# Eighteen unread matmuls between two groups of transposes, at three passages of a decoder kernel

## What is computed

```python
for layer in range(DEPTH):
    h = rms_norm(x, norm_mix[layer])
    proj = h @ w_in[layer]
    ...
    x = x + mix @ w_out[layer]
    h = rms_norm(x, norm_ffn[layer])
    if layer % 2 == 0:
        x = x + swiglu(h, ffn_w1[li], ffn_w3[li], ffn_w2[li])
    else:
        x = x + moe_swiglu(h, router[li], moe_w1[li], moe_w3[li], moe_w2[li])
```

## Time and profile before

| | us |
|---|---|
| median of 3 runs | 2078.56 |
| lowest, highest | 2078.51, 2080.9 |
| the profiled execution, its time | 2078.5 |
| the profiled execution, its span | 2076.7 |
| TensorE matmuls busy | 2023.9 (97%) |
| VectorE busy | 1583.8 (76%) |
| ScalarE busy | 1252.3 (60%) |

### The profile page before, as it was taken

The page is one execution under the profiler, slowest core; times in us unless marked ns, Lnnn a source line. Parts: engine busy times, 40 slices in busy tenths (PEclk is TensorE's granted clock), DMA queues, the critical chain, the costliest instruction groups (busy, mean ns, idle before and its releaser), DMA issues.

```text
span 2076.7 us, 28711 instructions
## 1 busy us (share of the span) xinstructions
PE 2023.9 (97%) x10743; PEld 1727.8 (83%) x10743; DVE 1583.8 (76%) x1219; ACT 1252.3 (60%) x1068; POOL 13.9 (1%) x21
## 2 busy tenths in 40 slices
PE   9999999999999999999979999999999999999997
PEld 8887888789998987888768888888888888888885
DVE  5778865755445778855767898888989888898986
ACT  5655455443345655454446777777777777777774
POOL 0000000000000000000000000000000000000000
PEclk9999999999999999999989999999999999999998
DMA  8523455255554523455238999999999999999994
GB/s 276 162 82 102 143 181 183 82 182 184 182 183 158 168 80 109 145 177 177 93 141 317 380 354 382 367 361 377 359 379 355 381 367 360 376 359 377 358 373 182
DMA packets 240494, 516.60 MB, mean 249 GB/s; under 512 B 11520, under 2 KB 34296, under 8 KB 240414
## 3 DMA queue, kind: packets, MB, share of 16 engines
q1 hardware_dynamic: 238018, 507.39, 69.1%
q0 software_dynamic: 2144, 7.88, 1.0%
q10 hardware_dynamic: 252, 0.22, 0.0%
HBM read 513.34 MB, written 2.12 MB: 248 GB/s over the span
## 4 chain that ended last, share of the span: by engine, by line
PE 91%; DVE 4%; ACT 2%; issue 2%; DVEq 0%; ACTq 0%
PE PS L481 27%; PE PS L483 26%; PE PS L482 26%; PE PS L565 7%; PE PS L1054 1%; ACT hi L1165 1%; PE PS L1031 1%; DVE lo L1652 1%; PE PS L806 1%; PE PS L720 0%; PE PS L1001 0%; PE PS L837 0%; DVE t_n L1675 0%; PE PS L1019 0%; DVE b_gc L1982 0%
## 5 line engine op out<-in xcount | busy, mean ns | idle before, releaser
L1652 DVE TENSOR_TENSOR lo<-raw,hi 128x2048 fp32r<-128x2048 f32 x481 | 1095.8, 2290 | 299.7 <-ACT hi L1165 297.5
L1165 ACT ACTIVATE hi<-raw 128x2048 fp32r<-128x2048 f32 x481 | 919.6, 1915 | 320.0 <-PE PS L483 313.8
L481 PE MATMUL PS<-hi,e_hi 128*128 128x512 f32 x896 | 356.2, 398 | 1.4 <-DVE e_lo L1675 1.4
L483 PE MATMUL PS<-hi,e_lo 128*128 128x512 f32 x896 | 350.4, 391 | 0.0
L482 PE MATMUL PS<-lo,e_hi 128*128 128x512 f32 x896 | 350.0, 391 | 0.0
L481 PE MATMUL PS<-hi,actT_hi 128*128 128x512 f32 x640 | 253.8, 397 | 3.7 <-DVE lo L1652 3.1
L483 PE MATMUL PS<-hi,actT_lo 128*128 128x512 f32 x640 | 249.7, 390 | 0.0
L482 PE MATMUL PS<-lo,actT_hi 128*128 128x512 f32 x640 | 249.2, 389 | 0.0
L481 PE MATMUL PS<-hi,fT_hi 128*128 128x512 f32 x536 | 208.8, 390 | 1.8 <-DVE fT_lo L1675 1.8
L483 PE MATMUL PS<-hi,fT_lo 128*128 128x512 f32 x536 | 208.7, 389 | 0.0
L482 PE MATMUL PS<-lo,fT_hi 128*128 128x512 f32 x536 | 208.7, 389 | 0.0
(11 more groups left out here) (324 smaller groups left out, 2147.1 us busy)
## 6 DMA issues: line engine op xcount, KB each, us to landing
raw<-in_moe_w SPq DMA_DIRECT2D x336, 1024.0 KB, 5.5
raw<-in_w_in SPq DMA_DIRECT2D x92, 1024.0 KB, 5.1
raw<-in_ffn_w SPq DMA_DIRECT2D x33, 1024.0 KB, 5.3
raw<-in_w_br SPq DMA_DIRECT2D x12, 1024.0 KB, 5.0
raw<-in_w_out SPq DMA_DIRECT2D x8, 1024.0 KB, 5.0
hankel<-hankel_dram POOLq DMA_DIRECT2D x1, 1536.0 KB, 12.8
x<-in_x SPq DMA_DIRECT2D x2, 512.0 KB, 5.1
f_gain<-in_norm_ffn POOLq DMA_DIRECT2D x2, 512.0 KB, 3.7
```

The source lines that it names most:

```text
L481: pe.matmul(out, a_hi, b_hi, start=first, stop=False, skip_group_check=True)
L483: return pe.matmul(out, a_lo, b_hi, start=False, stop=last, skip_group_check=True)
L1165: act.activation(hi[prog.u % SPLIT][:, :], raw[slot][:, :], COPY).then_inc(hi_made.sem, 1)
L1652: dve.tensor_tensor(lo[prog.u % RAW][:, :], raw[prog.u % RAW][:, :], hi[s][:, :].bitcast(F32), ALU.subtract).then_inc(lo_made.sem, 1)
```

## The change

`turn_input` calls a new helper between the first tile's eight transposes and the wait for the second tile's norm, in all calls but the first (`mixer(0)`). The helper issues eighteen matmuls. Their stationary operand is the first 128 columns of `ab_hi` (the high part of three small weight matrices, 192 columns, made near the start of the kernel), their moving operand all 192 columns. Each starts and ends its own sum, in bank 7 where `b` = 0 (place B) and in bank 1 where `b` = 4 (places A and C). They wait for nothing of their own, they signal nothing, and no instruction reads what they write.

```diff
@@ -501,6 +501,8 @@
             pe.wait_ge(norm_made.sem, norm_made.at(L, 3 * phase))
             for k in range(KT):
                 turn(0, k)
+            if L or phase:
+                spare(7 if b == 0 else 1, 18)
             for half in range(2):
                 pe.wait_ge(norm_made.sem, norm_made.at(L, 3 * phase + 1 + half))
                 for j in range(2 * half, 2 * half + 2):
@@ -554,6 +556,12 @@
+        def spare(b, count):
+
+            w = ab_hi[:, :, :, :].rearrange("p a k n -> p (a k n)")
+            for _ in range(count):
+                pe.matmul(PS[:, b, 0:3 * KT * 8], w[:, 0:P], w, start=True, stop=True)
```

## The result

The changed kernel takes 2088.38 us (median of 5 runs, 2087.1 to 2094.24) where the kernel before takes 2078.51 us (5 runs, 2077.45 to 2080.9): a ratio of 1.0051, with a 95% interval of 1.0037 to 1.0064. That is slower by more than the 0.2% that a measurement of this kernel can tell, and above the range that was given.

The account below looks back on a forecast made before the run. The prediction took the kernel as bound by TensorE, its matmuls busy for 97% of 2076.7 us. Terms -1.94 (A), +2.8 (B) and 0.0 (C) gave +0.9 on 2078.5, so 2079.4 us, range 2077.6 to 2083.0.

Parts of the forecast that it names:

- B: Layer 1, first norm: added matmuls delay the second tile's transposes and the first product; +2.8 us, bounds +1.2 to +5.7.
- A: Layer 0, second norm: added matmuls fill TensorE's idle time, the clock level stays up, products run faster; -1.94 us.
- C: Layer 1, second norm, before the router: narrow product done 1.2 us sooner, nobody gains; 0.0 us, 0.8 either way.
- The sum over the three places: Whole kernel: -1.94 + 2.8 + 0.0 = +0.9 us on 2078.5, so 2079.4 us, chance 0.47.
- The price of one matmul: Each added matmul at all three places: 0.119 us at the upper clock level, 0.213 us at the lower.
- the dear bound: Each added matmul priced per column: 0.160 us upper level, 0.320 us lower; as a rival 2080.3 us, chance 0.12.
- the estimate by the formula of the Trainium skill: Each added matmul: 160 ns cold, 82.5 ns warm; about 0.6 us off B's cost, not used in the sum.
- the level falls at A all the same: Rival at A: the clock level drops despite the added matmuls, A gives only 0.10 us; 2081.2 us, chance 0.22.
- the level does not rise: Rival at B: lower clock under the added matmuls; 2082.3 us with A kept (0.08), 2084.1 with A lost (0.05).
- The fast rival: From C on: level stays up to the gather, gather and 12 products save 5.8 us; 2073.6 us, chance 0.03.
- The forecast is wrong if...: Three signs: level at A falls before 449, is still low at B's first product, or is full at the gather.

Follow-up runs that it names:

- e6: The kernel before with 27 tiny matmuls (54 instructions) ahead of the expert loop; 2082.26 us, 73 pieces of code fetched.
- e8: The kernel before with 110 tiny matmuls (220 instructions) ahead of the expert loop; no total time given, steps with a loop return 127.44 and 127.60 us against 121.08.
- e14: The kernel before with 123 tiny matmuls (246 instructions) ahead of the expert loop; no total time given, no loss at the loop returns.
- e2: The change plus 74 tiny matmuls ahead of the expert loop, 256 added instructions in all; 2081.53 us, ratio 1.0003 to the kernel before.
- e4: The change without the matmuls at B, plus 92 tiny ones ahead of the expert loop, 256 added instructions; 2077.74 us, ratio 0.9996 to the kernel before.
- e10: The kernel before with 124 tiny matmuls (248 instructions) ahead of the expert loop; no total time given, 56 pieces fetched, no loss at the loop returns.
- e1: The kernel before with 54 tiny matmuls (108 instructions, as many as the change adds) ahead of the expert loop; 2089.09 us, ratio 1.0048.
- e3: The kernel before with 54 tiny matmuls behind the expert loop, ahead of the last scatter; 2078.77 us, ratio 0.9994.
- e5: The kernel before with 10 tiny matmuls (20 instructions) ahead of the expert loop; no total time given, placement found good.
- e7: The kernel before with 90 tiny matmuls (180 instructions) ahead of the expert loop; no total time given, nine pieces fetched per later pass.
- e9: The kernel before with 14 tiny matmuls (28 instructions) ahead of the expert loop; no total time given, first loop return costs, second does not.
- e13: The kernel before with 11 tiny matmuls (22 instructions) ahead of the expert loop; no total time given, placement found good.
- e15: The kernel before with only the change's eighteen at B, plus 110 tiny matmuls, 256 added instructions; 2081.48 us, ratio 1.0008.
- e11: The change without B, eight more matmuls behind A's second tile, both router waits filled, 256 added instructions; 2077.65 us, ratio 0.9991 to the kernel before.
- e12: Like e11, with 22 matmuls at B ahead of the first tile's wait and the gap behind the gather filled; 2076.57 us, ratio 0.9988 to the kernel before.

## Why the prediction was wrong

**The sum over the three places.** It said +0.9 us; the stages give -0.36 + 2.76 + 0.21 = +2.6 us. That alone would have been 2081, inside the range.

*The price of one matmul* was right: 0.119 us (2.24 us for 18, of which the last takes about 0.2), and the dear bound is out. So is the estimate by the formula of the Trainium skill ("TensorE: Matmul & The Clock Gate", section "Wait — 56ns, not 53.3ns?"), 82.5 ns.

*A* was forecast at -1.94 with the level kept, and the rival "the level falls at A all the same" at -0.10. The change's profile has the rival, softened: the level fell, at 449.2, later and for half as long, and the stage is 0.36 us shorter. Even that is not the eighteen's doing for certain: e6, e8 and e14, whose first column is like the change's and which have nothing added at A, are shorter by 0.3 to 0.4. Both cases exist for the same code, as e2 and e4 show with -1.83 and -1.86. Where nothing is added at A, the stage goes with the first column of the table: -0.3 to -0.4 us where that is -0.9 to -0.6 (e6, e8, e14), 0 where it is 0 (before, e10), -1.2 to -1.4 where it is +3.3 to +3.6 (e1, e3, e5), and +0.3 to +0.5 where it is +3.7 to +3.9 (e7, e9, e13, e15). So what the level costs at A goes with what happened 420 us earlier; that one causes the other was not tried. The step that failed at A was to take one execution's loss of 1.84 us as what stands to be gained each time.

*B* was right in mechanism: the eighteen stand in front of the second tile's transposes and push the first product back, forecast 2.9 us, measured 2.9. The size, +2.8 forecast, is +2.76 in the change, +2.77 in e15, and +4.0 in e2, where the lower level lasted longer (its eighteen took 4.13 us). That it fits so well is partly luck, for what the stage does without them is not fixed either: -0.15 us in e1 and e3, +0.2 in e6, e8 and e14, +1.7 in e7, e9 and e13. Set against kernels with a like start, the eighteen cost 2.5 us in the change and 1.1 in e15. The rival "the level does not rise" didn't occur in the change. In e2 it half did: all eighteen ran at the lower level, and it was up again only by the first product.

*C* was right: 0.0 at VectorE's read, gather and twelve products at the lower level as before. The fast rival (level kept up to the gather) failed, and e11 and e12 show that even the waits as filled there do not bring it.

**The failed step is one that was never written.** The sum ended with "-1.94 + 2.8 + 0.0", which says that nothing changes anywhere else. The eighteen were costed as time on TensorE and never as code. Three calls are 108 instructions ahead of a loop that is 1763 long and whose code just stayed in place, and the returns of the loop, +6.77 us, are more than twice the whole rest. No rival, bound or row covered it, and the statement "The forecast is wrong if..." looked at three places only: none of its three signs came true (the level at A fell at 449.2, just behind the 449 that it names), and the forecast was wrong all the same. The rows for it were there: the page before counted 55 pieces of code, and the table of queues for the loop had none of them. A loop whose fetches stop after the first pass stays in place, and a kernel with such a loop has something to lose.

The Trainium skill, "Runtime: NRT & Kernel Launch", section "Instruction fetch mechanics", says that TensorE's instruction memory is a FIFO of 128 KiB, refilled in blocks of 256 instructions. It also says that a taken branch whose target lies outside a window of two pages waits until the target is fetched. The traces agree with the blocks (1.20 MB in 73 pieces) and with a wait at a branch (6.28 us at the first return, of which 3.2 reach the matmuls). They disagree with the window: before, a loop of 6.89 blocks was repeated with no fetch at all. My estimate from the page's 128 KiB: that is eight blocks, and if one of them is being filled, a loop of up to seven would stay. That would be 30 placements, near the 33 to 63 that the scan shows, and e13 and e14 say that it is not the whole rule.

That the change's loss in the loop is the placement of the code is shown: e1 has the loss without the matmuls, e2 has the matmuls without the loss, e3 has the code behind and no loss. Why one return costs 1.8 us and another 5 to 6.5 the traces show for the most part. The 5.0 us at the change's first return are the stop of 3.2 us plus the lower level behind it (some 8 products at 0.2 us), while behind the second, shorter stop of 1.6 us its level stays up (granted clock 1.00). The three returns that cost some 5 us (the change's, e1's and e9's first) are those at which two pieces were on their way side by side. The cheap ones (the second of the change and of e1, both of e6 and of e7) have one at a time, and e8's two, the dearest, have the second stop. Why two pieces meet at some returns is open.

## What to carry to other kernels

Cost added instructions twice: as time on the engine, and as code ahead of each loop of that engine. Look in the table of queues whether the loop's later passes fetch code; where they don't, keep the number of instructions in front of the loop the same modulo one piece (here 256), or pad it, and check the count again after each edit. Put filling matmuls ahead of the wait whose idle time they are to fill, never between work and its waiting reader, and expect no more from them than the level's fall costs in an average execution, not in the one that was profiled.

## What the runs showed of the hardware

**A loop can be good or bad by its placement alone.** Loop of 1763 instructions: no fetch in its later passes at the five shifts tried from -10 to +22, nine pieces fetched per pass at 54, 108, 180 and 220. At 28 it was one pass of two. Price 3.7 to 13 us over two returns. The wait shows in the length of the branch: 0.21 us where nothing is fetched, 4.6 to 6.4 us where it is.

**The level at the kernel's start is chance.** The code there is the same in all kernels. Yet the stretch from 13 to 24 us has a granted clock of 0.84 before and of 0.55 in e2, so the lower level lasts 11 x 0.16 / 0.5 = 3.5 us in one and 11 x 0.45 / 0.5 = 9.9 us in the other. Before, and then e2:

```profile
13.00:24.00 11.00, 11.00 (x71) 8.64 (x70) 7.39 (x8) 7.51 (x13) 0.80 (x1) 0.84 0.83 271
```

```profile
13.00:24.00 11.00, 10.91 (x43) 7.28 (x44) 6.29 (x8) 6.09 (x14) 0.80 (x1) 0.55 0.83 263
```

71 matmuls started in one, 43 in the other, and all that follows is 3.6 us later. Together with the stages A and B, which go with it, it is why the runs of the kernel before spread from 2076.66 to 2085.01, and why effects of 2 to 3 us had to be read from the stages and not from the medians. Why none of e12's eleven runs was above 2077.61 I can't say.

**Matmuls of 8 columns by 8 are nearly free in time but not in code**: 60 of them took 1.75 us in e4, 0.029 us each, at the upper level. They left 3.65 us of the router's wait idle, and behind it the level was down, in the gather too.
